# Gate and up of a decoder layer by seven products of half blocks instead of eight, with weight sums made by adding DMAs

## The reference

```python
def swiglu_ffn(x, w_gate, w_up, w_down):       # D_MODEL 1024, D_FF 2816, SEQ 512
    h = jax.nn.silu(jnp.einsum('bsd,df->bsf', x, w_gate)) * jnp.einsum('bsd,df->bsf', x, w_up)
    return jnp.einsum('bsf,fd->bsd', h, w_down)
...
    h = layer_norm(DEEPNORM_ALPHA * h + mix, ln1_g[l], ln1_b[l])
    ff = swiglu_ffn(h, w_gate[l], w_up[l], w_down[l])
    h = layer_norm(DEEPNORM_ALPHA * h + ff, ln2_g[l], ln2_b[l])
```

## Time and profile before

| | us |
|---|---|
| time, median of 3 runs | 704.86 (704.56 to 704.95) |
| the profiled execution, its own time | 705.2 |
| span in its profile, first to last instruction | 703.4 |
| all before gate and up | 344.0 |
| four late slabs, in halves | 24.8 |
| loop over 40 slabs | 217.6 |
| down stage and second norm | 117.0 |
| mean granted clock of TensorE | 0.996 |

### The profile page before, as it was taken

One profiled execution on the slowest core, in us unless ns is written; L12 is line 12 of the kernel. 1 busy time (PEld: TensorE's weight loads), 2 busy tenths in 40 slices (PEclk: granted clock), 3 DMA queues, 4 the chain that ended last, 5 costly groups with the idle time before them and its releaser, 6 DMA issues.

```text
span 703.4 us, 9442 instructions
## 1 busy us (share of the span) xinstructions
PE 689.1 (98%) x3380; PEld 577.2 (82%) x3380; DVE 431.3 (61%) x739; ACT 336.7 (48%) x624; POOL 141.3 (20%) x129
## 2 busy tenths in 40 slices
PE   8999999999999999999999999999999999999985
PEld 6987888888888888888998888888888888888873
DVE  5569997767876236647923442233334337989897
ACT  5678787467766344333223222222222225677741
POOL 2110000000001000000236664355533415100000
PEclk9999999999999999999999999999999999999998
DMA  8221112211114522361357556654466433676643
GB/s 320 78 92 61 61 62 89 90 61 61 61 61 133 226 90 91 114 215 61 102 188 248 210 209 217 230 197 154 161 233 209 149 106 103 184 221 211 187 126 135
DMA packets 34723, 102.09 MB, mean 145 GB/s; under 512 B 3584, under 2 KB 3712, under 8 KB 34688
## 3 DMA queue, kind: packets, MB, share of 16 engines
q1 hardware_dynamic: 27504, 74.36, 31.8%
q0 software_dynamic: 7184, 27.27, 11.7%
HBM read 87.99 MB, written 13.63 MB: 144 GB/s over the span
## 4 chain that ended last, share of the span: by engine, by line
PE 88%; DVE 5%; ACT 3%; issue 1%; DMA 1%; POOL 0%; SPq 0%; DVEq 0%
PE ps L1376 22%; PE ps L1378 22%; PE ps L1377 22%; PE ps L1709 4%; PE ps L1711 4%; PE ps L1710 4%; PE ps L1458 2%; PE ps L1444 2%; PE ps L1414 1%; ACT rope L593 1%; DVE sl L857 1%; PE ps L1409 1%; DMA x_raw<-in_xT 1%; PE ps L1419 1%; DVE sl L849 1%
## 5 line engine op out<-in xcount | busy, mean ns | idle before, releaser
L857 DVE TENSOR_TENSOR sl<-raw,sh 128x512 fp32r<-128x512 f32 (+1 forms) x113 | 111.8, 989 | 77.2 <-ACT sh L807 77.2
L1376 PE MATMUL ps<-hTh,sh 128*128 128x512 f32 x320 | 124.5, 389 | 0.0
L1377 PE MATMUL ps<-hTh,sl 128*128 128x512 f32 x320 | 124.5, 389 | 0.0
L1378 PE MATMUL ps<-hTl,sh 128*128 128x512 f32 x320 | 124.5, 389 | 0.0
L807 ACT ACTIVATE sh<-raw 128x1024 fp32r<-128x1024 f32 x36 | 38.2, 1062 | 146.3 <-PE ps L1378 127.6
L849 DVE TENSOR_TENSOR sl<-raw,sh 128x1024 fp32r<-128x1024 f32 x50 | 61.8, 1236 | 54.7 <-ACT sh L577 54.5
L1376 PE MATMUL ps<-xh,sh 128*128 128x512 f32 x208 | 83.7, 403 | 0.0
L1378 PE MATMUL ps<-xl,sh 128*128 128x512 f32 x208 | 81.3, 391 | 0.0
L1377 PE MATMUL ps<-xh,sl 128*128 128x512 f32 x208 | 81.1, 390 | 0.0
L577 ACT ACTIVATE sh<-raw 128x1024 fp32r<-128x1024 f32 x50 | 52.8, 1058 | 42.8 <-PE ps L1378 36.4
L1378 PEld LDWEIGHTS ps<-hTl,sh 128*128 128x128 f32 x320 | 60.1, 188 | 12.6
(11 more groups left out here) (217 smaller groups left out, 1297.3 us busy)
## 6 DMA issues: line engine op xcount, KB each, us to landing
raw<-in_slabs SPq DMA_DIRECT2D x86, 512.0 KB, 3.3
stage<-in_wdn POOLq DMA_DIRECT2D x11, 1024.0 KB, 9.1
tw<-tsum POOLq DMA_DIRECT2D x11, 1024.0 KB, 5.7
raw<-tw SPq DMA_DIRECT2D x44, 256.0 KB, 2.8
raw<-in_wdn SPq DMA_DIRECT2D x33, 256.0 KB, 2.9
x_raw<-in_xT SPq DMA_DIRECT2D x8, 256.0 KB, 6.1
res<-in_x POOLq DMA_DIRECT2D x1, 2048.0 KB, 8.9
late_raw<-in_slabs SPq DMA_DIRECT2D x4, 512.0 KB, 4.2
```

Of the source, the lines that this page charges most:

```text
L857: return dve.tensor_tensor(dst, src, hi.bitcast(F32), ALU.subtract)
L1376: pe.matmul(dst, lh, rh, start=start, stop=False)
L1377: pe.matmul(dst, ll, rh, start=False, stop=False)
L1378: return pe.matmul(dst, lh, rl, start=False, stop=stop)
```

## The change

Gate and up of one column are seen as a 2 x 2 block product: the rows are gate and up, the inner dimension is cut into two halves of 512 channels, the tokens into two halves of 256. So the column's weights are A11, A12 (gate, first and second half of the channels) and A21, A22 (up), 128 x 512 each, and h is B11, B12, B21, B22. Eight block products become seven, by a Winograd form with sums of weight blocks (S1 to S4) and sums of blocks of h (V5 to V8). A product is four chunks of three matmuls with 256 moving columns. The first two of the 22 columns stay as they were (`FF_PLAIN`), the other 20 (`N_SEVEN`) are changed.

Per column: SP loads five blocks (A11, A22, A21, A12, A22) into one of two raw buffers of 10 KB a partition, GpSimd issues one DMA that adds A21 and A11 to the second and third of them (S1, S3). ScalarE splits seven blocks in four operations (`column_hi`), VectorE makes the low parts (`column_lo`) and two more sums (`s2`, `s4`). P1, P6, P7 and P4 gather in one bank, P5, P2 and P3 in another; between them ScalarE copies intermediate values out (`keep_x`, `keep_z`), VectorE adds (`up_right`, `gate`), ScalarE takes silu, VectorE multiplies (`hidden`, now two operations for such a column).

The sums of h are made once: ScalarE keeps h in float32 (`keep_h`, 8 copies), VectorE makes four sums (`v_sums`) and their low parts. The down weights' sums T1 to T4 are made in DRAM by GpSimd's DMAs alone (`t_sums`: a copy and three adding DMAs, each waiting for the one before): for seven pairs ahead of the load of x, for four behind it and ahead of the first `right_half`. `hidden_sums` moves from GpSimd to VectorE, the load of the second norm's gamma and beta behind the last product, and the down stage's split parts get other places (`ITEM_SLOT`). Sums are signed so that the result is the same.

```diff
+P1, P5, P6, P2, P7, P3, P4 = range(1, 8)
+SEVEN = 7
+X_BANK = (2, 4)
+YZ_BANK = (3, 5)
+HALF = SEQ // 2
+V5, V6, V7 = range(3)
+RAW_A11, RAW_S1, RAW_S3, RAW_A12, RAW_A22, RAW_BLOCKS = range(6)
+W_SLOT = {P1: 0, P5: 1, P6: 2, P7: 3, P2: 4, P3: 5, P4: 6}
+SPLITS = ((RAW_A11, 0, 2, P5), (RAW_S1, 2, 1, P6), (RAW_S3, 3, 2, P7), (RAW_A12, 5, 2, P4))
+ITEM_SLOT = (7, 0, 1, 2, 4, 3, 5, 6)
...
-        stage = at("stage", 0, [P, 4, 512])
-        tsum = at("tsum", 8, [P, 4, 512])
+        vt = at("vt", 0, [P, 3, 2, KC // 2, HALF], F32R)
+        hT_f = at("hT_f", 120, [P, KC, SEQ])
+        raw_f = [at("raw_f_even", 149, [P, RAW_BLOCKS, 512]), at("raw_f_odd", 191.5, [P, RAW_BLOCKS, 512])]
...
-            load_ring(LATE[-1] + 1, SLABS)
+            for k in range(N_SEVEN):
+                if k == 0:
+                    sp.wait_ge(lo_ready, N_FF)
+                elif k == 1:
+                    sp.wait_ge(hT_done, TB)
+                else:
+                    sp.wait_ge(split_lo, 4 * (k - 1))
+                sp.dma_start(raw_f[k % 2][:, :, :], gu[k][:, 0:RAW_BLOCKS, :]).then_inc(column_landed[k % 2], 16)
             for e in range(ITEMS):
                 p, i = divmod(e, PAIRS)
                 _, summed, w, _, _ = PRODUCTS[p]
                 if e == 0:
-                    sp.wait_ge(t_stored, 16 * PAIRS)
-                if e < DN_RAW:
-                    sp.wait_ge(lo_ready, ready(N_DN - 2) + e // 2)
-                else:
...
+            def flat(a):
+                return a.rearrange("q (a b) n -> q a (b n)", b=2)
+            def t_sums(i):
+                pool.dma_start(flat(tw[i]), flat(wdn[i])).then_inc(t_copied, 16)
+                pool.wait_ge(t_copied, 16 * (i + 1))
+                pool.dma_start(flat(tw[i, T1:T3 + 1]), flat(wdn[i, W12:W22 + 1]), accum_op=ALU.add,
+                               max_dma_last_dim=4096).then_inc(t_first, 16)
+                pool.wait_ge(t_first, 16 * (i + 1))
+                pool.dma_start(flat(tw[i, T2:T2 + 1]), flat(tw[i, T1:T1 + 1]), accum_op=ALU.add,
+                               max_dma_last_dim=4096).then_inc(t_second, 16)
+                pool.wait_ge(t_second, 16 * (i + 1))
+                pool.dma_start(flat(tw[i, T4:T4 + 1]), flat(tw[i, T2:T2 + 1]), accum_op=ALU.add,
+                               max_dma_last_dim=4096).then_inc(t_made, 16)
+            T_FIRST = 7
+            pool.wait_ge(slab_done, N_QF)
+            for i in range(T_FIRST):
+                t_sums(i)
...
             pool.wait_ge(res_landed, 48)
+            for i in range(T_FIRST, PAIRS):
+                t_sums(i)
             for k in RIGHT_BY_POOL[:-1]:
                 right_half(k)
-            pool.wait_ge(slab_done, N_FF)
+            for k in range(N_SEVEN):
+                pool.wait_ge(column_landed[k % 2], 16 * (k // 2 + 1))
+                pool.dma_start(raw_f[k % 2][:, RAW_S1:RAW_S3 + 1, :], gu[k][:, RAW_BLOCKS:, :], accum_op=ALU.add)\
+                    .then_inc(s13_made[k % 2], 16)
+            pool.wait_ge(product_done, SEVEN * N_SEVEN)
...
+            def column_hi(k, u):
+                first, at_slot, blocks, user = SPLITS[u]
+                if u == 0:
+                    act.wait_ge(s13_made[k % 2], 16 * (k // 2 + 1))
+                elif u == 1:
+                    act.wait_ge(s2_made, k + 1)
+                elif u == 3:
+                    act.wait_ge(s4_made, k + 1)
+                if k:
+                    act.wait_ge(product_done, SEVEN * (k - 1) + user)
+                elif u == 0:
+                    act.wait_ge(slab_done, N_FF)
+                act.activation(sh[:, 512 * at_slot:512 * (at_slot + blocks)],
+                               raw_f[k % 2][:, first:first + blocks, :].rearrange("p b n -> p (b n)"), ACT.Copy)\
+                    .then_inc(split_hi, 1)
+            def keep_x(k, q):
+                if q == 0:
+                    act.wait_ge(ff_done, k + 1)
+                act.wait_ge(product_done, SEVEN * k + (P6 if q else P1))
+                act.activation(sg[:, k % 2, q * HALF:(q + 1) * HALF], ps[:, X_BANK[k % 2], 0:HALF], ACT.Copy)\
+                    .then_inc(x_kept, 1)
+            def keep_z(k):
+                act.wait_ge(product_done, SEVEN * k + P5)
+                if k >= 2:
+                    act.wait_ge(up2_made, k - 1)
+                act.activation(zt[:, k % 2, :], ps[:, YZ_BANK[k % 2], HALF:SEQ], ACT.Copy).then_inc(z_kept, 1)
...
+            for k in range(N_SEVEN - 1):
+                column_hi(k, 3)
+                keep_x(k, 0)
+                keep_z(k)
+                column_hi(k + 1, 0)
+                keep_x(k, 1)
+                column_hi(k + 1, 1)
+                column_hi(k + 1, 2)
+                silu(k + FF_PLAIN)
+            k = N_SEVEN - 1
+            column_hi(k, 3)
+            keep_x(k, 0)
+            keep_z(k)
+            item_split(0)
+            keep_x(k, 1)
+            for e in range(1, 6):
+                item_split(e)
+            silu(FT - 1)
...
+            def v_sums(j):
+                b11, b12 = hT_f[:, 0:4, 0:HALF], hT_f[:, 0:4, HALF:SEQ]
+                b21, b22 = hT_f[:, 4:8, 0:HALF], hT_f[:, 4:8, HALF:SEQ]
+                if j == 0:
+                    dve.wait_ge(hT_kept, 2 * TB)
+                    dve.tensor_tensor(b11, b11, b12, ALU.subtract).then_inc(v_sum, 1)
...
+            def column_lo(k, u):
+                first, at_slot, blocks, _ = SPLITS[u]
+                dve.wait_ge(split_hi, 4 * k + u + 1)
+                cols = slice(512 * at_slot, 512 * (at_slot + blocks))
+                low(sl[:, cols], raw_f[k % 2][:, first:first + blocks, :].rearrange("p b n -> p (b n)"), sh[:, cols])\
+                    .then_inc(split_lo, 1)
+            def s2(k):
+                r = raw_f[k % 2]
+                dve.wait_ge(split_lo, 4 * k + 1)
+                dve.tensor_tensor(r[:, RAW_S1, :], r[:, RAW_S1, :], r[:, RAW_A11, :], ALU.add).then_inc(s2_made, 1)
+            def s4(k):
+                r = raw_f[k % 2]
+                dve.wait_ge(split_lo, 4 * k + 3)
+                dve.wait_ge(s2_made, k + 1)
+                dve.tensor_tensor(r[:, RAW_A12, :], r[:, RAW_S1, :], r[:, RAW_A12, :], ALU.add).then_inc(s4_made, 1)
...
+            def gate(k):
+                dve.wait_ge(product_done, SEVEN * k + P3)
+                dve.wait_ge(x_kept, 2 * k + 2)
+                dve.tensor_tensor(sg[:, k % 2, :], sg[:, k % 2, :], ps[:, YZ_BANK[k % 2], :], ALU.add)\
+                    .then_inc(gate_made, 1)
...
+                    k = f - FF_PLAIN
+                    dve.wait_ge(up2_made, k + 1)
+                    dve.scalar_tensor_tensor(out=h[:, HALF:SEQ], in0=up2[:, k % 2, :], scalar=-1.0,
+                                             in1=sg[:, k % 2, HALF:SEQ], op0=ALU.mult, op1=ALU.mult)
+                    dve.wait_ge(product_done, SEVEN * k + P4)
+                    dve.scalar_tensor_tensor(out=h[:, 0:HALF], in0=ps[:, X_BANK[k % 2], 0:HALF], scalar=-1.0,
+                                             in1=sg[:, k % 2, 0:HALF], op0=ALU.mult, op1=ALU.mult).then_inc(ff_done, 1)
...
+            column_lo(0, 0)
+            v_sums(0)
+            v_sums(1)
+            v_sums(2)
+            v_low(1, hT_f[:, 0:4, 0:HALF], vt[:, V5, 0, :, :], vt[:, V5, 1, :, :])
+            v_sums(3)
+            s2(0)
+            v_low(2, hT_f[:, 4:8, HALF:SEQ], vt[:, V6, 0, :, :], vt[:, V6, 1, :, :])
+            hidden(0)
+            column_lo(0, 1)
+            v_low(3, hT_f[:, 0:4, HALF:SEQ], vt[:, V7, 0, :, :], vt[:, V7, 1, :, :])
+            column_lo(0, 2)
+            s4(0)
+            hidden(1)
+            v_low(4, hT_f[:, 4:8, 0:HALF], hTh[:, 0:4, HALF:SEQ], hTl[:, 0:4, HALF:SEQ])
+            for k in range(N_SEVEN - 1):
+                if k:
+                    hidden(k + FF_PLAIN - 1)
+                column_lo(k, 3)
+                column_lo(k + 1, 0)
+                s2(k + 1)
+                if k % 2 == 0:
+                    hidden_sums(k // 2)
+                column_lo(k + 1, 1)
+                up_right(k)
+                column_lo(k + 1, 2)
+                gate(k)
+                s4(k + 1)
...
+                pe.wait_ge(hT_kept, r + 1)
...
-            with pe.Fori(1, FT // 2) as i:
-                for r in range(4):
-                    n = N_FF + r
-                    pe.wait_ge(lo_ready, i * 4 + ready(n))
-                    if r % 2 == 0:
-                        pe.wait_ge(ff_done, i * 2 + (r // 2 - 1))
-                    ff_slab(n + SPL, r // 2, r % 2, slice(0, SEQ), True)
+            left, right = slice(0, HALF), slice(HALF, SEQ)
+            upper, lower = slice(0, KC // 2), slice(KC // 2, KC)
+            def product(p, bank, cols, bh, bl, start):
+                for c in range(KC // 2):
+                    w = slice(W_SLOT[p] * 512 + c * P, W_SLOT[p] * 512 + (c + 1) * P)
+                    dst = ps[:, bank, cols]
```

(125 more changed lines are left out.)

161 lines of the change are left out of this document (91 added, 70 removed).

## The result

After the change the kernel takes 707.53 us (median of 10 runs, 706.16 to 709.78) against 704.96 (10 runs, 704.56 to 705.94): ratio 1.0038 [1.0027, 1.0049], 2.6 us slower. The forecast was 694.3, so faster by 10.6 us; the sign is wrong, though the time lies in the range of 688.5 to 709.0.

What follows compares the result with a forecast made beforehand. TensorE, busy for 98% of the span, was taken to bound the kernel. Gate and up: 217.6 - (204.0 + 2.0 + 1.0) = 10.6 us less; 705.2 - 10.6, less 0.3 to the median, 694.3 us; range 688.5 to 709.

Steps and rivals of the forecast that it cites:

- the buffers' loop: Raw buffers' two-column loop in gate/up: P7, splits, sums, hand-overs 9.7, load 5.4, adding DMA 5.0 us; 10.05 us a column.
- L: SP's load of 1.25 MB (five blocks) into a raw buffer: 5.1 to 5.6 us, taken as 5.4.
- A: GpSimd's adding DMA of 512 KB into a raw buffer: between 4.1 and 9.1 us, taken as 5.0.
- rival 2: Raw buffers' loop bounds gate and up: no net gain at A = 6.4 us, slower from there; chance 0.18.
- TensorE's gain: Gate and up: 84 matmuls at 0.120 make 10.08 us a column against 10.88; 16.0 us less over twenty columns.
- Rival 1: Nothing waits in gate and up (A at 4.1): 16.0 us less, 689 us; chance 0.14.
- TensorE's waits: Gate and up: nine waits a column instead of three, cost taken as 0.1 us a column, 2.0 in all.
- Rival 4: TensorE's waits in gate and up cost 0.56 us a column: 4 us less, 701 us; chance 0.09.
- The way in: Late slabs into the loop: keep_x late for the first P6 by 0.4 us; cost taken as 1.0 (0 to 3).
- DRAM sums: Down weights' sums as four dependent DMAs for each of 11 pairs: 17.9 us a pair, hidden, cost 0.
- Rival 3: DRAM sums late, TensorE waits for h ahead of 344 us; net slower from 24.8 us a pair; chance 0.09.
- strong form: DRAM sums' DMAs run on few engines: 36.4 us a pair, the kernel about 833 us; chance 0.03.

Runs made afterwards that it cites:

- e1: The changed kernel without its 20 adding DMAs, S1 and S3 left out, so it computes something else: 691.86 us, ratio 0.981 to the kernel before.
- e2: The changed kernel with each column's load in two DMAs, the first three blocks as soon as s4 is made: 690.17 us, again 690.20; 0.979 to the kernel before.
- e6: The changed kernel with its adding DMA cut into two dependent ones of 256 KB: 768.27 us, ratio 1.090 to the kernel before.
- e7: The changed kernel with S1 and S3 made by two GpSimd additions in SBUF instead of the adding DMA: 695.56 us, ratio 0.986 to the kernel before.
- e4: The kernel before with only the down weights' sums moved to adding DMAs in DRAM: 705.24 us, ratio 1.0002 to the kernel before.
- e3: The changed kernel with VectorE's hidden sums moved ahead of the next column's first low part: 705.62 us, ratio 1.0004 to the kernel before.
- e5: e2 with both ln2 loads issued behind GpSimd's last S3 sums of the down stage: 692.82 us, ratio 0.983 to the kernel before.

## Why the prediction was wrong

The step that failed is the sum for the buffers' loop, (9.7 + 5.4 + 5.0)/2 = 10.05 us, and with it the sentence that the loop and TensorE are level. The formula was the right one, but each of its terms was too small. In the turn shown above L is 6.06 us instead of 5.4 and A 5.76 instead of 5.0. The rest is 10.13 instead of 9.7: 9.85 on ScalarE and VectorE, and 0.28 until GpSimd issues, a hand-over that the 9.7 was to hold. That is 1.85 us a turn and 0.92 a column, 18 us over twenty columns, since above 10.08 nothing hides it. In time: the loop took 218.9 us against 204.0 + 2.0 + 1.0 = 207.0, the down stage 2.0 more, the part ahead of the loop 0.6 less; 694.3 + 11.9 + 2.0 - 0.6 = 707.6 us, and 707.5 was measured. It is rival 2's mechanism, which got 0.18. Its break-even of A = 6.4 held only with L at 5.4 and the rest at 9.7: L + A was to be 11.8, it was 11.82, and the rest came on top. That the result still fell in the range is no merit of the sum: the range was widened by that rival.

- **TensorE's gain.** 84 x 0.120 = 10.08 us a column is right: 10.09 in e1 and e2, where nothing waits. Rival 1 (689 us) is what e2 reaches, 690.2.
- **L.** Scaled from the 512 KB row at the queue's best rates, it got 5.1 to 5.6; the 20 loads took 5.8 and 6.0 (medians of the two buffers). Sharing isn't the reason: the loads at 322.45 and 353.95 us, with no other DMA issued beside them, took 5.9 each, as did e1's. So 0.79 MB more cost 2.6 us and not 1.8 to 2.3. The row of a smaller DMA plus bytes at a peak rate was no upper end.
- **A.** 5.0 was chosen between 4.1 and 9.1; the medians were 5.6 and 5.8, and 5.62 for the first one, which ran with no other DMA issued beside it. The rule of the Trainium skill (Collectives: The Full Stack, "The bandwidth ceiling: the fold count and why AG ≠ RS ≠ AR"), that an adding DMA reads two sources and in its collective ran at half the rate of a copy, gave an estimate of 5.7. The trace agrees with that number; no run shows the reason. That sentence priced the column at 10.4 us, still less than measured, since L was short too.
- **The rest of the loop.** 9.7 was forecast, 9.85 and the 0.28 measured, by another route: I took it through P7, the gate sum and `keep_x`, and it went through s2, the hidden sums and four low parts on VectorE. Near by luck, not by mechanism. The route through `keep_x` and P7 does show, in e6, where the stops were 6 us long.
- **Level limits.** For limits of 10.08 and 10.05 I took 10.2 and a range of 690 to 699. Each us of L + A is 0.5 a column, so 10 us in the end: the range had room for 0.5 us of error in two rows of which one wasn't in the trace.
- **TensorE's waits.** Forecast 2.0 us; in e1 and e2, with the same nine waits, the steps of the loop are above the pace by 0.26 us in all, at the first P6. Rival 4 is refuted.
- **The way in.** Forecast 1.0 lost. From the first late slab to the loop both kernels take 24.75 us, and the first P6 comes 0.26 us late, which is what the way in cost. The 0.6 us less lie ahead of the late slabs, where the profiles of the other runs scatter from 342.7 to 343.9 us; no gain is shown there.
- **VectorE beside GpSimd.** The low parts of 1024 took 1.22 to 1.24 us, as read from the earlier trace rows; with GpSimd adding again (e7) their mean is 1.40.
- **DRAM sums.** Forecast 17.9 us a pair, one behind the other. Measured from a pair's first issue to its last landing: 20.3 to 28.5. The copy took 7.1 us (5.7 by me), the first add 5.7 (5.0), the other two 4.4 each (3.6). But the next pair's copy isn't held by a pair's last add, so pairs started 16.6 to 20.3 us apart; the seven took 134 us (125 by me), the four 83 of their 95.6. The last landing was at 320.6, and GpSimd had been idle for 13.94 us when `right_half(0)` was asked for at 330.53. So the price was too low, and the cover held. Cost 0, shown by e4. Rival 3 falls; for its strong form the copy was to take 14.6 us. SP's slab loads rose from 3.3 to 4.6 us beside them, hidden as argued.
- **The hidden sums' move, off the path.** Wrong: two of its three sums, 0.74 of the 21.95 us turn, stand in the chain, and moving them freed only 0.32 us. Small all the same: e3's ratio of 1.0004 against 1.0038 is some 2.4 us.
- **The down stage, unchanged.** Wrong by 2.0 us. The last wait for `res` grew, and behind it came a lower clock (0.97 in this stage, 0.98 before). PE after, then before:

```profile
677.46 0.39 PE L1960 MATMUL ps<-sl,ah 128*128 128x512 f32 x1
680.95 0.66 PE L1958 MATMUL ps<-sh,ah 128*128 128x512 f32 x1 [3.11 <-DVE res L1462]
681.41 0.63 PE L1959 MATMUL ps<-sh,al 128*128 128x512 f32 x1
```

```profile
675.93 0.39 PE L1711 MATMUL ps<-sl,ah 128*128 128x512 f32 x1
678.19 0.47 PE L1709 MATMUL ps<-sh,ah 128*128 128x512 f32 x1 [1.88 <-DVE res L1297]
678.50 0.39 PE L1710 MATMUL ps<-sh,al 128*128 128x512 f32 x1
```

The gap is 3.49 instead of 2.26 us from start to start, and behind it eight matmuls go at 0.43 and not at 0.23, 1.6 us more; later stops that are shorter than before win some of it back. Why VectorE reaches `res` later stays open. VectorE is not idle in the 7 us ahead of it, before or after, so it has fallen behind earlier. The sums in DRAM aren't the reason: e4's wait is 1.9 us as before, its stage 117.4. In e2_split_load the stage takes 118.3 us, with 2.1 us of that wait and 1.3 for `sl`; there two loads of items took 6.3 and 6.5 us beside ln2's, but e5 shows that issuing these later doesn't help.

## What to carry to other kernels

Where a new load or DMA closes a loop over few buffers, write the loop as one sum and ask what one us more in each transfer does to the end: here 10 us, so two transfers known to 10% each could not carry the sign of a forecast. A buffer whose parts come free at different times should be reloaded by parts; 2.35 us of earlier start and 0.5 MB less in front of the dependent DMA turned a loss of 2.6 us into a gain of 14.8. Before moving an operation out of a chain, look for the wait that it covers.

## What the runs showed that was not expected

- An adding DMA of 512 KB took 5.6 to 5.8 us (medians), of 256 KB 4.2 to 4.4, so half the bytes cost three quarters of the time; issued beside a load of 1.25 MB the 256 KB took 6.9 to 7.5 (e6). Between the landing that GpSimd waited for and its next issue lie 0.28 us.
- A wait of TensorE of 3.1 to 3.6 us in the down stage (after, e1, e3, e6) was followed by matmuls of 512 columns 0.43 us apart, the lower of the two clock levels (granted clock of the stage 0.97, 0.96, 0.96, 0.97); behind waits of 1.9, 2.1 and 2.4 us (before, the two runs of e2) none were. The waits of 2.9 us (e7) and 2.8 us (e5) differ: behind the first some were, behind the second none (0.97 and 0.99).
- The four dependent DMAs within DRAM, 2 MB moved or added, took 20.3 to 28.5 us from first issue to last landing and started 16.6 to 20.3 us apart; over 11 pairs they cost TensorE nothing (e4).
- The low parts of 1024 beside GpSimd's additions have a mean of 1.40 us in e7, and its `hidden` operation of 128 x 256 takes 1.33 us where it took 0.43 after: such additions are not free for VectorE, though the version is still 12 us faster than after.
